# Two conv tiles instead of three as packed matmuls on TensorE, the other two tiles' 62 taps on VectorE

## The reference

```
h = rmsnorm(x, mix_pre_norm);  u = h @ w_in              # 1024 -> 3072
u_a, u_b, hq, hk, hv, hg = columns of u, 512 each
y_conv = silu(layernorm(depthwise_conv31(u_a * sigmoid(u_b)) + dw_b))
y_ret  = silu(hg) * norm(retention(rotary(hq), rotary(hk), hv))
y = concat(y_conv, y_ret) @ w_out
```

## Time and profile before

| | before |
|---|---|
| runs, median (lowest to highest) | 921.55 us (919.61 to 921.73) |
| the profiled execution, its own time | 922.56 us |
| its span in the trace | 920.7 us |
| TensorE matmul / weight load busy | 902.0 us (98%) / 812.3 us (88%) |
| VectorE / ScalarE / GpSimd busy | 654.3 us (71%) / 506.9 us (55%) / 310.5 us (34%) |
| granted TensorE clock, mean | 0.998 |

### The profile page before, as it was taken

How to read it: one execution, slowest core, us unless ns; L and a number is a source line. 1 busy time by engine, 2 the same in 40 slices (tenths; PEclk the granted TensorE clock), 3 DMA queues, 4 the chain that set the end, 5 groups by cost and what they waited for, 6 DMA issues and landing times.

```text
span 920.7 us, 16451 instructions
## 1 busy us (share of the span) xinstructions
PE 902.0 (98%) x6876; PEld 812.3 (88%) x6876; DVE 654.3 (71%) x807; ACT 506.9 (55%) x750; POOL 310.5 (34%) x117
## 2 busy tenths in 40 slices
PE   8999999999999999999999999999999999999997
PEld 7998886888888878999999989998999788888886
DVE  4986667888883257658798765867655589999623
ACT  7534737544554456655656565555555466666532
POOL 4000000566565410000000005846784155666542
PEclk9999999999999999999999999999999999999999
DMA  9693463655556544445545445443455455555551
GB/s 356 220 282 110 149 222 114 236 183 183 189 188 219 183 167 156 181 152 200 199 139 184 160 94 185 142 153 125 153 203 171 161 182 186 190 190 189 186 198 46
DMA packets 32298, 163.99 MB, mean 178 GB/s; under 512 B 9154, under 2 KB 11602, under 8 KB 13794
## 3 DMA queue, kind: packets, MB, share of 16 engines
q1 hardware_dynamic: 32162, 162.89, 52.2%
q0 software_dynamic: 64, 0.08, 0.0%
HBM read 161.40 MB, written 1.57 MB: 177 GB/s over the span
## 4 chain that ended last, share of the span: by engine, by line
PE 84%; DVE 8%; DMA 4%; ACT 2%; issue 1%; SPq 1%; DVEq 0%; ACTq 0%
PE ring L1699 27%; PE acc L1799 17%; PE acc L1731 9%; PE ring L1731 9%; PE acc L1732 5%; PE ring L1732 5%; PE ring L1750 4%; DVE w_lo L1116 2%; DMA u<-uconv 2%; DMA raw<-wstream 2%; PE acc L1851 1%; PE acc L1999 1%; PE acc L1812 1%; DVE ret_inv L1303 1%; ACT w_hi L689 1%
## 5 line engine op out<-in xcount | busy, mean ns | idle before, releaser
L641 POOL TENSOR_TENSOR w_lo<-raw,w_hi 128x1024 fp32r<-128x1024 f32 x101 | 290.3, 2877 | 587.8 <-ACT w_hi L689 587.7
L689 ACT CAST w_hi<-raw 128x1024 fp32r<-128x1024 f32 x284 | 296.8, 1051 | 312.0 <-PE ring L1699 125.1
L1116 DVE TENSOR_TENSOR w_lo<-raw,w_hi 128x1024 fp32r<-128x1024 f32 x183 | 228.9, 1264 | 113.8 <-ACT w_hi L689 103.5
L1699 PE MATMUL ring<-h,w_hi 128*128 128x256 f32 x1376 | 251.6, 285 | 1.7 <-DVE h L1193 1.7
L1699 PEld LDWEIGHTS ring<-h,w_hi 128*128 128x128 f32 x1376 | 214.8, 192 | 4.6 <-issue 4.1
L1699 PE MATMUL ring<-h,w_lo 128*128 128x256 f32 x688 | 195.0, 283 | 0.1
L1699 PEld LDWEIGHTS ring<-h,w_lo 128*128 128x128 f32 x688 | 132.1, 192 | 0.3 <-issue 0.3
L1731 PE MATMUL acc<-h,w_hi 128*128 128x512 f32 x352 | 126.1, 400 | 0.8 <-DVE h L1193 0.8
L1731 PE MATMUL ring<-h,w_hi 128*128 128x512 f32 x352 | 124.2, 395 | 0.0
L1732 PE MATMUL acc<-h,w_lo 128*128 128x256 f32 x352 | 99.6, 283 | 0.0
L1732 PE MATMUL ring<-h,w_lo 128*128 128x256 f32 x352 | 98.9, 281 | 0.0
(11 more groups left out here) (277 smaller groups left out, 1278.6 us busy)
## 6 DMA issues: line engine op xcount, KB each, us to landing
raw<-wstream SPq DMA_DIRECT2D x142, 1024.0 KB, 5.0
u<-uconv SPq DMA_DIRECT2D x4, 426.0 KB, 10.2
toep_t<-toep SPq DMA_DIRECT2D x16, 96.0 KB, 3.2
x<-x_tok SPq DMA_DIRECT2D x2, 512.0 KB, 4.7
mem<-mem_tok SPq DMA_DIRECT2D x1, 1024.0 KB, 11.6
w_ple<-wproj SPq DMA_DIRECT2D x1, 1024.0 KB, 7.3
out_t<-y SPq DMA_DIRECT2D x4, 256.0 KB, 2.2
decay<-decay_tab SPq DMA_DIRECT2D x1, 768.0 KB, 6.5
```

What stands on the lines that cost most here:

```text
L641: nc.gpsimd.tensor_tensor(w_lo[:, u % UNITS], unit_of_raw(u), as_f32(w_hi[:, u % UNITS]), ALU.subtract).then_inc(lo_ready["pool"], 1)
L689: nc.scalar.copy(w_hi[:, u % UNITS], unit_of_raw(u)).then_inc(hi_ready, 1)
L1116: V.tensor_tensor(w_lo[:, u % UNITS], unit_of_raw(u), as_f32(w_hi[:, u % UNITS]), ALU.subtract).then_inc(lo_ready["dve"], 1)
L1699: last = mm(dst, w[a], src[:, b, kt], start=n == 0 and i == 0, stop=n == kts - 1 and i == 2)
```

## The change

Tile 1 moves from TensorE to VectorE. `PACKED` holds tiles 2 and 3 only, so `conv_packed` runs twice, GpSimd makes two weight products, the store and the four loads carry two tiles, and ScalarE copies two. VectorE now has 62 taps, of tiles 0 and 1: seven instead of four in each of the eight fills `conv` and `qk` (56), four ahead of `v` 0's low parts, and again up to four (two are left) ahead of `v` 1's.

```diff
-PACKED = (1, 2, 3)
+PACKED = (2, 3)
...
                 wait_read(dve, "conv", j)
                 tiles_in[0] = j + 1
-                taps(4)
+                taps(7)
...
             for j in range(4):
                 feed_behind("qk", j)
-                taps(4)
+                taps(7)
             dve.wait_ge(load_side, 48)
             rope_of(0, q_raw)
             rope_of(1, k_raw)
...
             V.tensor_scalar(lb[:, 5], lb[:, 4], -1.0, 1.0, ALU.mult, ALU.add).then_inc(lb_ready, 1)
+            taps(4)
             feed_behind("v", 0)
             turned_lo("mem", 0)
+            taps(4)
             feed_behind("v", 1)
             turned_lo("mem", 1)
```

## The result

The changed kernel takes **924.88 us** (median of 9 runs, 923.16 to 927.11), the kernel before 921.55 (9 runs, 919.61 to 923.02): ratio **1.0043**, 95% interval 1.0028 to 1.0059. It is slower by 0.4%. The forecast was 922.5 us, within 0.3% of before, and I gave "within" 0.80 of the chance. 924.88 us lies just inside the range given (919.8 to 925.0), but the loss is about three and a half times the one forecast, and it is clear of the noise. The profiled execution took 923.70 us around a span of 921.9.

The account below looks back on a forecast made before the run. TensorE's matmuls (902.0 of 920.7 us) bound the kernel; its saved 3.52 and 0.54 us are eaten by waits of 1.27 and 3.7 us, so +1.0 on 921.55 gives 922.5 us, range 919.8 to 925.0.

Parts of the forecast that it names:

- alternating taps, step: VectorE from conv 2 on: taps alternating between two tiles step by 0.40 us, ends 0.34 and 0.52.
- the two low parts at 21 us: VectorE at 21.08 us: without GpSimd's third weight product, conv_in of tile 0 starts at 23.79 instead of 25.51, gain 1.72 us.
- VectorE's shift at the rotary: Sum of VectorE's shifts fill by fill: rotary starts 4.26 us later, at 68.13 instead of 63.87.
- wait of TensorE at `qk` 0: TensorE waits 1.27 us for unit 8's low part, which ends at 38.02 and is wanted at 36.80.
- wait of TensorE ahead of the mean: TensorE stands at the mean at 80.8 and waits 3.7 us for VectorE's last tap.
- start of the mean: Mean over channels starts at 84.5 against 83.49 before, set by VectorE's last tap: +1.0 us.
- Rival 1: VectorE's alternating taps are no faster: 40 steps of 0.12 us more, 4.8 us, total 927.3 us; chance 0.08.
- Rival 2: GpSimd's second product holds VectorE as the third did: no 1.72 us gain, +2.7, 924.3 us; chance 0.10.
- Rival 3: VectorE keeps up, steps 3.6 us shorter in all: mean at 80.8 or 79.5, 917.6 to 918.9 us; chance 0.06.
- So +1.0 goes to the end: Behind the mean the order is as before, a 2.2 us margin stays, so the +1.0 us reaches the end.
- costed at nothing: One packed-tile copy less on ScalarE, later store and reload of conv_in, weight slots free up to 5.9 us later: no cost.
- others: Chance 0.04 left for outcomes besides the forecast (0.72) and the three rivals.

Follow-up runs that it names:

- again: The changed kernel run again with nothing edited, beside the kernel before: 924.93 us, ratio 1.0038.
- after_3: The changed kernel, unedited, run once more as the measure for the fourth set: 924.28 us, ratio 1.0035.
- even: The changed kernel with taps dealt 7, 4, 7, 7 at the conv fills and 8 at each qk fill: 924.43 us, ratio 1.0030.
- before_pad: The kernel before with 32 small matmuls added at the wait for mem's fourth turned tile: 924.95 us, ratio 1.0029.
- after_pad_mem: The changed kernel with 32 small matmuls at TensorE's wait for mem's fourth turned tile, behind the mean: 922.51 us, ratio 1.0023.
- skip_pad_mem: skip with 32 small matmuls at the wait for mem's fourth turned tile; output lacks tile 1's convolution: 917.76 us, ratio 0.9951.
- late_even_split: late_even with 16 small matmuls at TensorE's first wait and 16 at the wait for mem's fourth tile: 918.01 us, ratio 0.9968.
- late_even: rope_late with taps dealt 7, 4, 7, 7, then 8 per qk fill, last 5 behind qk 3: 919.71 us, ratio 0.9994.
- rope_late: The changed kernel with the last six taps right behind qk 3, k's rotary sum and lb behind the mean's subtraction: 920.7 us, ratio 1.0009.
- skip: The kernel before with tile 1's convolution left out except one tap, on both engines; output incomplete: 920.43 us, ratio 1.0000.
- pad: The changed kernel with 32 small matmuls in TensorE's wait ahead of the mean: 926.0 us, ratio 1.0058.
- both: The changed kernel with tile 1 done twice: VectorE's taps into a scratch tile, TensorE packing three tiles as before: 924.87 us, ratio 1.0030.
- warm: The changed kernel with 28 matmuls of 128 columns in TensorE's wait ahead of the mean: 924.71 us, ratio 1.0038.
- after_pad16: The changed kernel with 16 small matmuls at the wait for mem's fourth turned tile: 923.22 us, ratio 1.0019.

## Why the prediction was wrong

**The plan of the first 100 us held, nearly term by term.**

| term | predicted | measured |
|---|---|---|
| packed matmuls | 7.05 us | 7.11 |
| alternating taps, step | 0.40 us | seven and a low part in 2.78, so 0.40 |
| the two low parts at 21 us | 2.71 | 2.73 (start to `conv_in`: 2.71) |
| VectorE's shift at the rotary | +4.26 | +4.11 (68.88 - 63.87 - 0.90) |
| wait of TensorE at `qk` 0 | 1.27 | 0.1, in `again` 2.2, in `after_3` 0.8 |
| wait of TensorE ahead of the mean | 3.7 | 3.41, in `again` 1.94, in `after_3` 3.39 |
| end of the last tap to the mean | 0.06 | 0.14 (85.17 to 85.31) |
| start of the mean | 84.5 | 84.41 (85.31 - 0.90) |
| shift handed on at the root | +1.0 | +1.17, in `again` +1.16 |

Rival 1 (taps no faster when they alternate) fell: the step is 0.40, not 0.52, so the rule of the Trainium skill that I set beside it ("VectorE: DVE Perf Modes", the rules for kernel authors: the count of chained operations matters, not their semaphores) doesn't decide here. A tap that needs the last one pays 0.12 us more than one that doesn't. Rival 2 (GpSimd's second product holds VectorE as the third did) fell by the 2.73 us. Rival 3 fell: VectorE didn't keep up. The waits of TensorE are uneven: what it doesn't wait at `qk` 0 it waits ahead of the mean, 3.6 to 4.2 us in all for 5.0 predicted. That doesn't matter, since VectorE sets the mean either way. The range had no sum of its own: its ends are 920.1 and 924.3 us widened by 0.3 and 0.7, though the spread named for it was 2.1; that 924.88 falls inside is luck.

**The step that failed is "So +1.0 goes to the end".** It takes for granted that everything behind the mean is the same program, merely later. It isn't: it stands 64 matmul records nearer to the start of TensorE's instructions. That opened a stop of 1.1 to 1.5 us 400 us further on, where the kernel before has one of 0.3 us; against it the changed kernel loses 1.0 to 1.4 us there. What I had costed at nothing were ScalarE's copy, the transfers of data and the weight slots; the transfers of instructions were not on the list. I gave "others" 0.04. The test that I wrote down for being wrong, the mean at 84.5 and the end moving by something else, is what came.

**How far the sum reaches.** The changed kernel was measured three times: 1.0043, 1.0038, 1.0035, in the mean 3.6 us. From the traces come 1.2 us at the mean (1.6 against the second trace of before) and 1.0 to 1.4 of stop, 2.2 to 3.0. For the rest there are three candidates, and the runs don't settle their shares.
- *Half clock.* The granted clock over the runs of the changed kernel is 0.9954, 0.9953 and 0.9956 in the mean (9, 12 and 12 runs), against 0.9975 for the kernel before beside the last two (33 and 35 runs). A stretch of 3.4 us at half clock is 1.7 / 920 = 0.0018 of it, so by this estimate an execution has about one more. Ten traces have the changed kernel's taps ahead of the rotary; five have it at 38 to 43 us, behind the wait at `qk` 0, where it costs nothing since VectorE is behind (`again` has the same +1.16), and three at 83 to 91, behind the wait ahead of the mean, where it cost 1.6 us (`after_3`) to 3.0 (`even`). None of the three traces of the kernel before, padded or not, has one at either place (728 twice, 107 in `before_pad`). Three in ten at some 2.3 us is 0.7 us.
- *More than one stop's worth.* The sum of root, stop and small matmuls against the time measured: with the place of before, `after_pad_mem` +1.7 and +2.1, `skip_pad_mem` -4.0 and -4.5, `late_even_split` -3.1 and -2.9; with the stop, `late_even` -2.1 and -0.6, `rope_late` -1.0 and +0.8, `skip` -3.4 and 0.0, `before_pad` +1.6 and +2.7. So the kernels with the stop seem slower than their sums. But not all fit: `pad`, without it, is 1.5 us above its sum (+3.8 and +5.3), and `both` and `warm` are 1.2 and 2.2 us below (+4.0 and +2.8, +5.7 and +3.5). Giving the place back took 1.5 us (changed kernel), 1.6 and 3.0 (`late_even`) and 4.5 (`skip`), though it costs 0.5. One traced execution shows one stop of 1.1 to 1.5 us; that other executions stop longer would fit, and isn't shown.
- *Two rates of the stage `up`.* Executions differ in a stage that the change doesn't touch. In the first block the matmuls of `up` (line 1733, from 154 us on) take 122.1 us in 13 of the 20 traces and 124.4 in 7, in the second block 2.3 us less or more likewise (9 traces and 11), added evenly over the stage. The changed kernel shows both: 122.1 us in the first trace, 124.4 in `again` and `after_3`. A half-clock stretch at 728 us, in six traces, costs some 1.5 us more. That is up to 6 us between two executions of one kernel, about the spread of the runs, and it is why a whole span of one trace can't be set against another. Whether a kernel changes how often each rate comes isn't known; part of the rest, and of the differences in the point above, may be that.

So what the change does in the first 100 us costs 1.2 to 1.6 us by the traces, close to the +1.0 forecast; the padding that takes the stop away costs 0.5 more, and `after_pad_mem` with both measured 2.1 (0.4 to 3.9 by its interval).

**What the change could have given.** The prediction's picture that VectorE's order sets the mean leads to `rope_late`: the same 62 taps, placed ahead of the rotary, put the mean where TensorE is ready for it. With the taps of `late_even` and the place kept, that is worth 0.2 to 0.4% over the kernel before (0.9977, 0.9968, 0.9961). The change as made gives TensorE's 3.5 us away to a wait; with a better order it keeps 2 to 3.6.

## What to carry to other kernels

Taking work off the bound engine shortens the span only if the receiving engine's order lets the next meeting point move; here the taps were put ahead of that point and the rotary, which nobody there waits for, was too. When a kernel with thousands of TensorE instructions changes their number, look in the waits view for "issue" in the middle of a fill: the place of every later instruction in its blocks has shifted. Here the stop itself is 0.1% of the time, and giving the place back moved the time by 0.2 to 0.5%. Look at the weight loads too, where the small stop of the kernel before shows. The control is cheap: give the same number of tiny matmuls back inside a wait, ahead of the stop, and see whether it goes. And before a remainder of 1 or 2 us is explained, several traces of one kernel must be compared: here one untouched stage alone differed by 2.3 us between them.

## What the hardware showed that I had not expected

- TensorE stood once per execution at the same place within a block of its instructions, 1 to 27 records behind 128 matmul records of 32 columns in 1.2 us, and went on 2.2 to 2.8 us after a packet of instructions had started: 1.1 to 1.5 us at a shift of half a block either way, 0.85 at a quarter, 0.4 at 8 records, 0.1 to 0.4 at zero.
- The clock of TensorE fell to half for 3.4 or 6.8 us in or behind single waits: of 2.2 us at `qk` 0 (`again`), of 3.4 (`after_3`) and 4.6 (`even`) ahead of the mean. Behind the same waits other executions kept the full clock (the first trace of the changed kernel waited 3.41 us and ran the mean in 1.97, `after_pad16` 3.40 us). Filling a wait with small matmuls didn't prevent it: `pad` had it there, and three of the five traces with all 32 at `mem`'s fourth tile have it at 103 to 110 us.
- The same stage of the same kernel ran at two rates in different executions, 122.1 and 124.4 us.
- A tap of 256 elements steps by 0.52 us when it needs the one before it and by 0.40 when it needs the last but one.
- A low part that began beside GpSimd's product lasted 2.93 us, and ended 1.08 us after it; with the third product away the pair of low parts takes 2.73 us instead of 4.51, though GpSimd's first two products still run (18.70 to 22.49 in the changed kernel).
